# Two expert layers: 104 instead of 96 of 256 tokens by gathered rows, with their indices, token rows and head sums through TensorE

## What is computed

```python
q = (xt @ wq).reshape(t, 8, 2, 128)
scores = einsum('thcd,hcnd->thcn', q, sub_keys)          # 8 heads, two halves, 128 keys each
sv, si = top_k(scores, 16)
cand_s = sv[:, :, 0, :, None] + sv[:, :, 1, None, :]     # 256 candidates a head
best_s, best_p = top_k(cand_s, 16)
idx = take_along_axis(si0 * 128 + si1, best_p)           # 128 experts of 16384 a token
gate = softmax(best_s)
act = einsum('td,thkd->thk', x, u_tab[idx])
y = einsum('thk,thkd->td', gelu(act) * gate, v_tab[idx])
```

## Time and profile before

| | before |
|---|---|
| median of 3 runs | 2206.39 us (2198.05 to 2209.8) |
| the profiled run | 2208.4 us, of it 2206.6 us from the first instruction to the last |
| TensorE busy | 2136.2 us, 97% |
| VectorE / GpSimd / ScalarE busy | 1221.4 / 560.3 / 458.5 us |
| DMA | 616.27 MB, mean 279 GB/s |
| granted TensorE clock | 0.989 of full |

### The profile page before, as it was taken

How to read it: one execution, slowest core, us unless ns; L and a number is a source line. 1 busy time by engine, 2 the same in 40 slices (tenths; PEclk the granted TensorE clock), 3 DMA queues, 4 the chain that set the end, 5 groups by cost and what they waited for, 6 DMA issues and landing times.

```text
span 2206.6 us, 32029 instructions
## 1 busy us (share of the span) xinstructions
PE 2136.2 (97%) x13280; PEld 1915.6 (87%) x13280; DVE 1221.4 (55%) x2451; ACT 458.5 (21%) x1071; POOL 560.3 (25%) x446
## 2 busy tenths in 40 slices
PE   7998899999999999989999999999999989999999
PEld 3465688888678999989999998668999989999999
DVE  3235621222653997879644444662997779744443
ACT  3013410001241124433100000251224434100000
POOL 0000000000000075445433332000065455443332
PEclk9999999999999999999999999999999999999999
DMA  9324143444424599999999997433589999999996
GB/s 373 145 93 165 39 172 134 172 142 182 149 81 155 197 361 374 397 352 402 410 408 404 407 408 292 153 115 134 179 349 379 394 339 404 409 409 409 408 408 272
DMA packets 114330, 616.27 MB, mean 279 GB/s; under 512 B 10249, under 2 KB 11657, under 8 KB 96138
## 3 DMA queue, kind: packets, MB, share of 16 engines
q1 hardware_dynamic: 56394, 403.31, 46.8%
q0 software_dynamic: 57504, 208.82, 24.9%
q10 hardware_dynamic: 288, 2.10, 0.3%
HBM read 612.16 MB, written 2.03 MB: 278 GB/s over the span
## 4 chain that ended last, share of the span: by engine, by line
PE 86%; DMA 5%; DVE 4%; ACT 1%; issue 1%; POOL 0%; ACTq 0%; DVEq 0%
PE psum L425 85%; DMA arena<-in_peer_u,small 5%; PE psum L483 1%; DMA arena<-in_peer_v 1%; PE psum L531 0%; DVE arena L2072 0%; DVE arena L2081 0%; POOL arena L2220 0%; DVE arena L1615 0%; ACT HT L1178 0%; DVE arena L1603 0%; DVE arena L2096 0%; DVE arena L1877 0%; DVE small L1857 0%; DVE arena L1866 0%
## 5 line engine op out<-in xcount | busy, mean ns | idle before, releaser
L425 PE MATMUL psum<-arena 128*128 128x160 f32 (+5 forms) x6362 | 978.1, 316 | 24.3 <-ACT arena L1350 18.0
L425 PEld LDWEIGHTS psum<-arena 128*128 128x128 f32 (+1 forms) x6362 | 903.2, 191 | 80.7 <-issue 31.1
L425 PE MATMUL psum<-HT,arena 128*128 128x160 f32 (+1 forms) x5472 | 874.9, 320 | 9.6 <-ACT HT L1178 5.6
L425 PEld LDWEIGHTS psum<-HT,arena 128*128 128x128 f32 x5472 | 823.0, 191 | 47.6 <-issue 10.0
L2121 DVE SCALAR_TENSOR_TENSOR arena<-arena,small 128x1024 f32<-128x1024 f32 x180 | 231.3, 1285 | 296.0 <-DMA arena<-in_peer_v,small 292.5
L2220 POOL DMA_INDIRECT arena<-in_peer_v,small x192 | 222.8, 1161 | 356.8 <-PE psum L425 282.1
L2220 POOL DMA_INDIRECT arena<-in_peer_u,small x192 | 249.7, 1301 | 247.1 <-DVE small L2072 190.4
L2231 POOL TENSOR_TENSOR arena<-arena 128x512 f32<-128x512 f32 x12 | 15.4, 1282 | 839.9 <-ACT arena L1207 839.7
L2072 DVE CUSTOM_DVE_ANT_0 arena<-arena 128x1024 f32<-128x1024 f32 x168 | 199.5, 1220 | 37.6 <-DMA arena<-in_peer_u,small 36.0
L425 PE MATMUL psum<-arena,HT 128*128 128x384 f32 (+3 forms) x544 | 194.6, 515 | 0.5 <-ACT HT L1098 0.4
L425 PEld LDWEIGHTS psum<-arena,HT 128*128 128x128 f32 x544 | 103.6, 193 | 82.4 <-issue 33.5
(11 more groups left out here) (244 smaller groups left out, 1111.0 us busy)
## 6 DMA issues: line engine op xcount, KB each, us to landing
arena<-in_peer_ut SPq DMA_DIRECT2D x64, 2048.0 KB
arena<-in_peer_v SPq DMA_DIRECT2D x64, 2048.0 KB
arena<-in_w_mod SPq DMA_DIRECT2D x12, 2048.0 KB
arena<-in_w_in SPq DMA_DIRECT2D x16, 1536.0 KB
arena<-in_w_up SPq DMA_DIRECT2D x11, 2048.0 KB
arena<-in_peer_wq SPq DMA_DIRECT2D x8, 2048.0 KB
arena<-in_w_out SPq DMA_DIRECT2D x6, 2048.0 KB
arena<-in_w_down SPq DMA_DIRECT2D x11, 1024.0 KB
```

The costliest lines, as they stand in the source:

```text
L425: return pe.matmul(o, a, b, start=start, stop=stop, skip_group_check=True)
```

## The change

104 tokens go by gathered rows, in six full groups of 16 tokens and a seventh of 8 (16 partitions a token, 8 steps): ROWS becomes 104, the dense way has 152 columns and 38 gate batches. Value gathers are paced to 96 steps over 30 tiles.

- **Indices:** TensorE multiplies the indices with selecting matrices `CHOOSE` (made by GpSimd from the identity), one product a group, behind score pair 5. VectorE picks with `OWN` and `OWNH` the head that belongs to the partition (`pick_indices`, between `choose(1)` and `choose(0)`).
- **Token rows:** ScalarE replicates a group's columns of `HT` 8 (16) times into `XNG` (`replicate`), TensorE transposes them (`spread_rows`), ScalarE copies the result over `XNG`; groups after pairs 0, 1, 27, 34, 42, 50 and 58. The store, the spreads and the first transposes are gone.
- **Head sums:** TensorE transposes the row sums `YP` of a group into the lower banks (`row_values`), VectorE sums over the heads there and adds to `XT` (`row_heads`), one group late, the last one between the final adds.
- The gates still go through `bounce`, in two reads for one.
- **Front:** the root `heads_rooted` moves into the loop, ahead of the last tile's copies.

Cut to its core:

```diff
-ROW_TOKENS = 96
+ROW_TOKENS = 104
 TD = T - ROW_TOKENS
 GTOK = P // PH
-RGROUPS = ROW_TOKENS // GTOK
-ROWS = RGROUPS * TOPK
+HTOK = GTOK // 2
+FULL = ROW_TOKENS // GTOK
+RGROUPS = FULL + 1
+FULL_TOKENS, FULL_ROWS = FULL * GTOK, FULL * TOPK
+ROWS = FULL_ROWS + TOPK // 2
...
+def values_before(m):
+
+    n = m - ROWS - VALUE_LEAD
+    return 0 if n < 0 else n * (XQ - 2) // (ROWS - VALUE_LEAD) + 1
...
+        IDX_AFTER = 5
+        SPREAD_AFTER = [0, 1, 27, 34, 42, 50, 58]
...
+                        if 2 * q + a in SPREAD_AFTER:
+                            spread_rows(SPREAD_AFTER.index(2 * q + a))
+                        if 2 * q + a == IDX_AFTER:
+                            row_indices()
...
+                def spread_rows(g):
+
+                    pe.wait_ge(s("replicated"), since("replicated") + g + 1)
+                    for half in range(2):
+                        transposes(f"xn{g}{half}", [XNG[:, g % 2, (4 * half + j) * P:(4 * half + j + 1) * P]
+                                                    for j in range(4)], banks=UPPER)
+
+                def row_indices():
+
+                    pe.wait_ge(s("idx_ready"), since("idx_ready") + 4)
+                    pe.wait_ge(s("chooser"), since("chooser") + 2)
+                    for half in range(2):
+                        ps = begin(f"ix{half}", UPPER)
+                        for j in range((4, RGROUPS - 4)[half]):
+                            last = mm(ps[:, j * NSEL:(j + 1) * NSEL],
+                                      CHOOSE[:, half * 4 + j, :], EIDX[:, NSEL:2 * NSEL], True, True)
+                        end(last, f"ix{half}")
...
-                            last = mm(psum[4 + m // 2][:, (m % 2) * T:(m % 2) * T + TD], w[:, a, m * P:(m + 1) * P],
-                                      WA[:, i, :], i == 0 and m % 2 == 0, False)
-                    last.then_inc(s("v_used"), 1)
-                    tile["last"] = (s("v_used"), since("v_used") + q + 1)
+                            last = mm(psum[4 + m // 2][:, (m % 2) * TD:(m % 2 + 1) * TD], w[:, a, m * P:(m + 1) * P],
+                                      WA[:, i, :], i == 0 and m % 2 == 0, i == XTILES - 1)
+                            if i == XTILES - 1 and m % 2 == 1:
+                                if m == KC - 1:
+                                    used_up.append(tile)
+                                end(last, f"y{m // 2}")
...
                 def row_values(g):
 
                     pe.wait_ge(s("yp_ready"), since("yp_ready") + g + 1)
-                    for m in range(KC):
-                        c = (m % 2) * T + TD + g * GTOK
-                        last = mm(psum[4 + m // 2][:, c:c + GTOK], YP[g % 4][:, m * P:(m + 1) * P], SELG,
-                                  False, g == RGROUPS - 1)
-                        if g == RGROUPS - 1 and m % 2 == 1:
-                            end(last, f"y{m // 2}")
-                    if g < RGROUPS - 1:
-                        last.then_inc(s("yp_used"), 1)
-
-                for half in range(2):
-                    transposes(f"xn{half}", [HT[:, 4 * half + j, TD:T] for j in range(4)], rows=ROW_TOKENS,
-                               banks=UPPER)
+                    for half in range(2):
+                        transposes(f"rv{g}{half}", [YP[g % 4][:, m * P:(m + 1) * P]
+                                                    for m in range(4 * half, 4 * half + 4)], banks=LOWER)
...
-                due = [(g + 1) * XQ // RGROUPS + 2 for g in range(RGROUPS - 1)]
+                due = [values_before(ROWS + group_rows(g)[-1]) + 3 for g in range(RGROUPS - 1)]
...
-            root("heads_rooted", small[:, 0:64], lambda: act.wait_ge(s("heads_mean"), 1))
+                    root("heads_rooted", small[:, 0:64], lambda: act.wait_ge(s("heads_mean"), 1))
...
+                def replicate(g):
+
+                    if g >= 2:
+                        act.wait_ge(s("rows_used"), since("rows_used") + (g - 1) * TOPK - POOL_ROWS)
+                    n = group_tokens(g)
+                    own = HT[:, :, TD + g * GTOK:TD + g * GTOK + n]
+                    act.activation(XNG[:, g % 2, :].rearrange("p (c t h) -> p c t h", c=KC, t=n),
+                                   bc(own.unsqueeze(3), P, KC, n, P // n),
+                                   ACT.Copy).then_inc(s("replicated"), 1)
+
+                act.wait_ge(s("l_normed"), since("l_normed") + 4)
+                replicate(0)
+
+                def rows_spread(g):
+
+                    jobs.wait_full(act, f"xn{g}1")
+                    for half in range(2):
+                        copy_out(f"xn{g}{half}", XNG[:, g % 2, half * 512:(half + 1) * 512],
+                                 bank(f"xn{g}{half}")[:, :])
...
+                    if m in SPREAD_AFTER:
+                        rows_spread(SPREAD_AFTER.index(m))
+                    if m + 1 in SPREAD_AFTER:
+                        replicate(SPREAD_AFTER.index(m + 1))
...
-                        steps(dve.tensor_scalar(BA[:, own], BA[:, own], base[:, 0:1], None, ALU.add))
-                        dve.tensor_copy(EIDX[:, own].bitcast(U32), BA[:, own]).then_inc(s("idx_ready"), 1)
+                        dve.tensor_scalar(EIDX[:, own], BA[:, own], base[:, 0:1], None, ALU.add
+                                          ).then_inc(s("idx_ready"), 1)
...
+                def pick_indices():
+
+                    for half in range(2):
+                        ps = reading(f"ix{half}")
+                        n = (4, FULL - 4)[half]
+                        at = half * 4 * NSEL
+                        last = dve.tensor_tensor(
+                            PICK[:, at:at + n * NSEL].rearrange("p (g h k) -> p g h k", h=PH, k=TOPK),
+                            ps[:, 0:n * NSEL].rearrange("p (g h k) -> p g h k", h=PH, k=TOPK),
...
+                    steps.later(dve.tensor_reduce(
+                    steps(dve.tensor_reduce(
+                    dve.tensor_copy(EG.bitcast(U32), ACTV).then_inc(s("idx_picked"), 1)
...
+                pick_indices()
                 for t in range(4):
...
+                def row_heads(g, half):
+
+                    n = group_tokens(g)
+                    ps = reading(f"rv{g}{half}")
+                    summed = rstd[:, 1, half * 64:half * 64 + 4 * n]
+                    dve.tensor_reduce(summed, ps[:, :].rearrange("p (c h) -> p c h", h=P // n), AX.X, ALU.add
+                                      ).then_inc(free(f"rv{g}{half}"), 1)
+                    jobs.wait_read(dve, f"rv{g}{half}")
+                    x = XT[:, 4 * half:4 * half + 4, TD + g * GTOK:TD + g * GTOK + n]
+                    steps(dve.tensor_tensor(x, summed.rearrange("p (a t) -> p a t", a=4), x, ALU.add))
...
+                    row_sums(g * TOPK, len(group_rows(g)))
+                    if g:
+                        row_heads(g - 1, 0)
+                        row_heads(g - 1, 1)
                 for g in range(4):
+                    if g % 2 == 0:
+                        row_heads(RGROUPS - 1, g // 2)
                     ps = reading(f"y{g}")
-                    x = XT[:, 2 * g:2 * g + 2, :]
-                    dve.tensor_tensor(x, ps[:, :].rearrange("p (a t) -> p a t", a=2), x, ALU.add
+                    x = XT[:, 2 * g:2 * g + 2, 0:TD]
...
-                        if m >= ROWS + VALUE_LEAD:
-                            pool.wait_ge(s("v_used"), since("v_used") + (m - ROWS - VALUE_LEAD) // (ROWS // XQ) + 1)
-                        if m < ROWS and m % TOPK == RING - 1 and TOPK < m < (RGROUPS - 1) * TOPK:
-                            spread_rows(m // TOPK + 1)
+                        if values_before(m):
+                            pool.wait_ge(s("v_used"), since("v_used") + values_before(m))
...
-                    jobs.wait_read(pool, f"xn{half}")
-                pool.dma_start(row_tokens, XNS[0:ROW_TOKENS, :]).then_inc(s("rows_moved"), 16)
-                pool.wait_ge(s("rows_moved"), layer * (16 + RGROUPS * 16) + 16)
-                pool.sem_inc(tick, 1)
-                spread_rows(0)
-                spread_rows(1)
                 jobs.wait_read(pool, "sc03")
-                pool.wait_ge(s("idx_ready"), since("idx_ready") + 4)
-                move_out(0, EIDX, "idx_moved")
-                move_in(0, EG, "idx_moved")
-                pool.wait_ge(s("idx_moved"), layer * 32 + 32)
+                last = P - HTOK
+                pool.tensor_copy(CHOOSE[:, 0:FULL, :].rearrange("p g (t h) -> p (g t) h", h=PH),
+                                 bc(IDENT[:, P - ROW_TOKENS:last].unsqueeze(2), P, FULL_TOKENS, PH)
+                                 ).then_inc(s("chooser"), 1)
+                pool.tensor_copy(CHOOSE[:, FULL, :].rearrange("p (t h) -> p t h", t=HTOK),
+                                 bc(IDENT[:, last:P].unsqueeze(2), P, HTOK, 2 * PH)
+                                 ).then_inc(s("chooser"), 1)
+                pool.wait_ge(s("idx_picked"), since("idx_picked") + 1)
```

93 lines of the change are left out of this document (57 added, 36 removed).

## The result

The changed kernel takes 2213.06 us in the median of 17 runs (2202.47 to 2215.83), the kernel before 2202.49 in 17 runs beside them (2195.71 to 2210.36): ratio 1.0043, 95% interval 1.003 to 1.0057. That is 10 us slower, where I had forecast 2 us faster. The time lies in the range, and within the 0.5% that I gave the largest chance; the sign and the sum are wrong. Part of it is the base: my sum was made against a profiled run of 2208.4 us, and the median of before's 17 runs is 6 us less. The profiled run of after took 2214.46 (span 2212.5 against 2206.6).

What follows compares the result with a forecast made beforehand. TensorE and DMA were taken to tie in the expert layers. +2.3 us for each of two layers and -6.5 us in the front gave -1.9 us, 2204 us on the median; range 2188 to 2222.

Steps and rivals of the forecast that it cites:

- Part 5: End of each expert layer: head sums through TensorE, last transposes replacing last sums; even, bounds -1 and +2 us.
- the one-hot wait: Gated score part: TensorE's wait of 9.6 us for VectorE's one-hot chain should not return; 1 us left.
- Part 3: Gated score part: without token-row spreads through memory, slow DMA stretches go; 14 us less DMA against 10 us added.
- Part 4: Score stage: indices through TensorE start gathers 4 us earlier, but VectorE's picking delays the other token block's selections.
- the new wait: Before the selections, TensorE waits for VectorE's gates: 5 us a layer, bounds 0 and 9, plus 2 us half clock.
- Rival A: Before the selections, the wait for gates does not come: 5 + 2 us a layer less, 2190 us; chance 0.22.
- Part 2: Value stage: 8 more gathered rows make DMA the bound; 119.5 MB at 408.5 GB/s take 292.5 us.
- rival B: Value stage not bound by DMA: TensorE's 271 us for 302, 30 us a layer less, 2144 us; chance 0.05.
- Part 1: Scores and values: 152 dense columns instead of 160 save 14 us a layer in each, if TensorE sets the pace.
- Part 6: Front, once: root moved into the loop removes TensorE's 5.7 us wait; -6.5 us, bounds -5 and -8.
- Rival C: Gated score part: slow stretches are not the spreads' doing and stay; 10 us a layer more, 2224 us; chance 0.17.
- faster by more: Whole kernel: faster by more than about 0.5% (11 us); chance 0.28.

Runs made afterwards that it cites:

- s2: Changed kernel with dense sums added ahead of the last group's head sums and the last full group's transposes one tile earlier; 2206.68 us, ratio 1.0016 to before.
- s1: Kernel before with only ScalarE's root for the head scales moved into the loop of copies; 2194.15 us, ratio 0.9966.
- s11: Kernel before with the four late spreads of each layer reading 128 different expert-table rows, same bytes and packets; 2185.22 us, ratio 0.9909 to before.
- s7: Kernel before with the four late spreads of each layer cut to 8 of 1024 columns; 2187.28 us, ratio 0.9928.
- s5: Changed kernel with TensorE's index products behind score pair 4 instead of 5; 2202.95 us, ratio 1.0007 to before.
- s3: Changed kernel loading only three quarters of each weight tile of the value stage; 2141.6 us, ratio 0.9726 to before.
- s4: Changed kernel with 96 gathered tokens instead of 104, six groups and no half group; 2189.36 us, ratio 0.9946 to before.
- s8: Changed kernel with 96 tokens, index products behind pair 4 and dense sums ahead of the last head sums; 2187.1 us, ratio 0.9928 to before.
- s10: Changed kernel, 104 tokens, index products behind pair 4, dense sums ahead of last head sums, last full group's transposes before the last tile; 2201.23 us, ratio 0.9997 to before.

## Why the prediction was right or wrong

**Part 5, head sums: wrong, and the step that failed.** "At the end, the last transposes (0.87) replace the last sums and two pieces of 1 us on VectorE come between the adds: even, bounds -1 and +2." It measured +3.9 and +3.7 us, 7.6 in all, against a miss of 7.8 between the profiled runs. Set like against like, as below the table, the end of a layer has 6.8 of the 7.8: 5.0 behind the last sums or transposes and 1.8 in the second group of transposes. I followed one group past the last tile and not two, counted the pieces by one group, and did not ask what stands behind them on VectorE: the dense sums, then the next layer's weighting or the output. One reading of the order in which VectorE takes its work at the end would have found it. s2, which changes that order and the tile behind which the last full group's transposes stand, takes back 4.2 us in its trace; the rest of the ends is read from the traces and not tested.

**The base: wrong.** The sum starts from a run of 2208.4 us, and the median of 17 is 2202.5; the changed kernel's profiled run lies 1.4 above its median. That is 4.5 of the 12.5 us between the forecast and the measured difference of the medians. s1's trace shows a likely cause, the one-hot wait of 1.4 and 5.9 us where I had 8.4 and 9.6. I gave "bounds 0 and 9.6" to what would remain of it in after and none to what there was before.

**Part 3, spreads: right.** No slow stretch at full DMA share, no wait for the one-hot chain, and s11 shows the cause. Under the 380 GB/s that I had named lie the ten microseconds from 850, 920 and 960 in layer 0 (328, 378 and 376) and those from 1690 in layer 1 (287), at shares of 0.95, 0.97, 0.98 and 0.82. Its size in the median is 15 us over the two layers (s7), though there the transposes that replace the spreads are absent. The gated part took 208.6 us in layer 1 against 212.8 forecast; the value stage starts at 1896.6 (forecast 1899.3).

**Part 4, the new wait: right in place and mechanism.** Forecast 5 us a layer and 2 of half clock; 5.26 and 2.4 in layer 0. In layer 1 only 1.13 us show because TensorE was late itself; the selections come at 1688.1 instead of the 1686.5 forecast. s5 gives it back: 10 us in all. Rival A is out. The first gather goes at 1614.12, 2.6 us earlier than before and not 4.

**Part 2, value stage by bytes: right.** Forecast DMA end 2191.8; the rate falls away then (291, 180 and 53 GB/s in the three microseconds from 2191), VectorE takes the last row at 2195.7, beside the last tile's matmuls, and the stage ends at 2202.3 with its transposes (forecast 2201.1). A tile takes 9.7 us from start to start (1922.85 to 1932.58) where I had 9.2, the first three tiles of the stage being there without a wait; the total of the bytes held. Rows and tiles do not quite end together, as I had feared, but that costs nothing. Layer 0 is 2 us worse. s3 shows that with fewer bytes it falls from 304 to 269 us, which puts rival B out as a forecast and confirms its 271 us as TensorE's bound. The Trainium skill's page "DMA: Bandwidth & Descriptors" (Specifications) gives about 358 GB/s as a core's HBM limit; the trace moved 408 over 294 us and the measurement decides. Its 435 GB/s for the fabric was reached by no such stretch either.

**Part 1: size right, its worth wrong.** Two score pairs, the matmuls of one tile, take 8.27 us from start to start (1888.37 to 1896.64) where I had 8.26. But s4 shows where it went. With the waits away (s5 beside s8) the score stage gains 12.6 us, and the value stage returns 18 us, since there DMA was at its limit already at 96 tokens: over 5 us lost a layer. My sum contained this trade, yet never stated it alone; asked for in s4's expectation, I had it as even.

**Part 6: right.** -7.6 in the changed kernel's trace, -6.3 in that of s1 (forecast -6.5, bounds -5 and -8); the median of s1 is 8.6 us lower, with an interval of 3 to 12.

**Rival C** alone had the sign (2224), and its mechanism did not occur: no wait for the one-hot chain. The limit that I gave it was wrong too. It was to decide "as soon as the average of the gated part is below 411"; the average was 405, and TensorE stood still for 0.1 us. The time fell in the range by other losses, that is, by luck.

**A slip in the chances.** The three terms named for "faster by more" (B, two thirds of A, a tenth of the forecast) add up to 0.25, and not to 0.28.

## What to carry to other kernels

When a sum of saved and added work comes out near nothing, look at how the work behind a stage's last instruction is queued on each engine, and at whether the profiled run is a typical one, the two things that decided here: look at a wait in a second run before booking it as a gain. Split a change that trades two resources into its halves before judging it; here the root (-8.6 us) and freedom from the spreads (-15 us) were worth having, and the eight tokens (+24 us as built, +14 with the wait and the order at the end mended, s10 beside s8) hid both. The two gains do not simply add: s4, which has both, gained 13 us and not 24, and the difference is what the new paths cost, or scatter. And before a path through memory is replaced, ask what in it is slow: writing copies so that no address is read twice took one DMA, and beat the reworked path by 11 us.

## What the runs showed of the hardware

Reading 64 KB of DRAM eight times in one transfer of 128 packets of 4 KB brought the DMA rate of all queues together down to 309 to 354 GB/s for about 10 us at full DMA share; as many bytes from distinct addresses left it at 414 to 421 (s11). In the value stage, where rows and weight tiles both move in packets of 4 KB, the rate is 409 GB/s at a share of 1.03 from 1950 to 2000 in every trace, whether TensorE waits for tiles there (the changed kernel) or not (before, s3). Not expected either: in layer 0 of the changed kernel the granted clock was 0.50 from 1.9 us before the end of a wait of 5.3 us until 4.9 us behind it. Behind the wait of 1.1 us in layer 0 of s5 the selections and the next tile took their times of full clock (0.87 and 8.43 us), so that shortening the wait by 4 us paid 6.2 us of score stage in that layer (316.9 to 310.7).
